# Attention in an encoder layer: the mask in the bias table, values on two column halves, the copy ahead of the exponentials, the sink as a column of scores

## The reference

```python
m = jnp.maximum(jnp.max(s, axis=-1, keepdims=True), sb)
p = jnp.exp(s - m)
denom = jnp.sum(p, axis=-1, keepdims=True) + jnp.exp(sb - m)
...
s = jnp.einsum('brjchd,bjkhd->bhjrck', qb, kb).astype(jnp.float32) * scale + bias[None]
s = jnp.where(valid[None, None], s, NEG_INF)
p = jax.nn.softmax(s, axis=-1).astype(v.dtype)
```

## Time and profile before

| | us |
|---|---|
| median of three runs | 2774.3 |
| the profiled execution, its own time | 2770.2 |
| its span (first to last instruction) | 2768.4 |
| TensorE matmuls busy in the span | 2559.1 |
| VectorE busy | 1794.7 |
| ScalarE busy | 1459.1 |
| GpSimd busy | 253.4 |

### The profile page before, as it was taken

How to read it: one execution, slowest core, us unless ns; L and a number is a source line. 1 busy time by engine, 2 the same in 40 slices (tenths; PEclk the granted TensorE clock), 3 DMA queues, 4 the chain that set the end, 5 groups by cost and what they waited for, 6 DMA issues and landing times. The chain is left out here.

```text
span 2768.4 us, 41766 instructions
## 1 busy us (share of the span) xinstructions
PE 2559.1 (92%) x15442; PEld 2295.4 (83%) x15442; DVE 1794.7 (65%) x2743; ACT 1459.1 (53%) x2028; POOL 253.4 (9%) x280
## 2 busy tenths in 40 slices
PE   7999978888797499999999999999999999999992
PEld 5888756666675499999999999999999999999991
DVE  6354277676556766676676666766767667667675
ACT  4332344444464356556565565565655655556553
POOL 0000033221000101001001010010110100101100
PEclk9999989999898699999999999999999999999996
DMA  4332212221542567677677676776776767767765
GB/s 151 124 122 92 102 44 72 71 76 50 212 144 95 203 229 250 222 255 247 225 254 245 234 245 223 255 245 225 254 240 241 242 227 252 247 226 251 243 239 210
DMA packets 97210, 538.73 MB, mean 195 GB/s; under 512 B 10800, under 2 KB 17200, under 8 KB 46576
## 3 DMA queue, kind: packets, MB, share of 16 engines
q1 hardware_dynamic: 89744, 511.82, 52.0%
q0 software_dynamic: 7392, 25.96, 4.2%
HBM read 499.99 MB, written 37.75 MB: 194 GB/s over the span
## 5 line engine op out<-in xcount | busy, mean ns | idle before, releaser
L1415 DVE TENSOR_TENSOR ex_w_lo<-ex_w,ex_w_hi 128x2048 fp32r<-128x2048 f32 x387 | 886.9, 2292 | 471.2 <-ACT ex_w_hi L1368 455.9
L1368 ACT ACTIVATE ex_w_hi<-ex_w 128x2048 fp32r<-128x2048 f32 x387 | 739.2, 1910 | 232.6 <-PE ex_down_ps L1519 114.1
L1501 PE MATMUL ex_gate_ps<-ex_xt,ex_w_hi 128*128 128x384 f32 x2048 | 594.3, 360 | 1.5 <-DVE ex_xt L1421 1.5
L1501 PE MATMUL ex_up_ps<-ex_xt,ex_w_hi 128*128 128x384 f32 x2048 | 592.1, 359 | 0.0
L1503 PE MATMUL ex_gate_ps<-ex_xt,ex_w_lo 128*128 128x192 f32 x2048 | 513.8, 251 | 0.0
L1503 PE MATMUL ex_up_ps<-ex_xt,ex_w_lo 128*128 128x192 f32 x2048 | 512.7, 250 | 0.0
L1503 PEld LDWEIGHTS ex_gate_ps<-ex_xt,ex_w_lo 128*128 128x128 f32 x2048 | 392.6, 192 | 0.6
L1503 PEld LDWEIGHTS ex_up_ps<-ex_xt,ex_w_lo 128*128 128x128 f32 x2048 | 391.2, 191 | 0.0
L1501 PEld LDWEIGHTS ex_gate_ps<-ex_xt,ex_w_hi 128*128 128x128 f32 x2048 | 385.8, 188 | 2.3 <-issue 1.7
L1501 PEld LDWEIGHTS ex_up_ps<-ex_xt,ex_w_hi 128*128 128x128 f32 x2048 | 384.3, 188 | 0.0
L630 ACT ACTIVATE at_probs<-at_probs,at_neg_top 128x384 f32<-128x384 f32 (+1 forms) x192 | 109.6, 572 | 178.7 <-DVE at_neg_top L684 109.7
(11 more groups left out here) (213 smaller groups left out, 4406.9 us busy)
## 6 DMA issues: line engine op xcount, KB each, us to landing
ex_w<-in_w_experts SPq DMA_DIRECT2D x387, 1024.0 KB, 4.8
pj_w<-in_w_in SPq DMA_DIRECT2D x54, 512.0 KB, 3.5
at_bias<-in_near_bias SPq DMA_DIRECT2D x8, 1536.0 KB, 7.3
pj_x<-in_x SPq DMA_DIRECT2D x12, 512.0 KB, 4.5
o_scratch<-at_o SPq DMA_DIRECT2D x24, 256.0 KB
mx_o<-o_scratch SPq DMA_DIRECT2D x12, 512.0 KB, 3.8
mx_x<-in_x SPq DMA_DIRECT2D x12, 512.0 KB, 4.5
acc_scratch<-mx_x SPq DMA_DIRECT2D x12, 512.0 KB, 5.4
```

The source lines that it names most:

```text
L1368: act.activation(w_hi[:, c % SLOTS, :], w[:, c % SLOTS, :], ACT.Copy).then_inc(hi_w, 1)
L1415: dve.tensor_tensor(w_lo[:, c % SLOTS, :], w[:, c % SLOTS, :], w_hi[:, c % SLOTS, :].bitcast(F32), ALU.subtract).then_inc(lo_w, 1)
L1501: nc.tensor.matmul(out[:, b, 0:2 * CAP], w_hi[:, slot, f], xt[:, k, :, :].rearrange("p h c -> p (h c)"), start=k == 0, stop=False)
```

## The change

- The table of biases that is put together on the host now holds -1e30 wherever a key is not seen. The mask tensor, its loads and GpSimd's additions are gone; VectorE waits for the load of the bias.
- The additions write to a new tile `raw`, eight rows of 385 elements, whose last column holds the head's sink. The exponential reads from `raw` and writes to `probs`; for a window unit it takes one column more, so its sum contains the sink. The separate subtraction, exponential and addition for the sink are gone. `probs` has four slots in place of six.
- The scores go around three PSUM banks in place of one for each head.
- Weighing is turned round: the 64 columns of a head's values are the stationary operand and the turned probabilities the moving one. The two heads write to PSUM partitions 0 to 63 and 64 to 127 of one bank, that is, each uses one half of the array's columns (`tile_position`), and their matmuls alternate.
- The result lies as features by queries, so ScalarE copies it to SBUF (`o_turn`), TensorE transposes it into another bank, and VectorE scales from there, one turn of the loop later (u-3).
- ScalarE's order is now: copy of the output of u-3, copy of the turned probabilities of u-1, exponentials of u.
- The turned values have one PSUM bank in place of two.

```diff
@@ -501,11 +501,10 @@
         N = len(units)
-        window_units = [sum(x[0].window for x in units[:u]) for u in range(N)]
...
-        PROBS, STATS, FLIPS, OUTS, BIASES, V_SLOTS = 6, 4, 6, 2, 3, 2 * len(V_TILES)
+        PROBS, STATS, FLIPS, BIASES, V_SLOTS, SCORES = 4, 4, 6, 3, 2 * len(V_TILES), 3
...
@@ -515,34 +514,31 @@
-        mask = sb("at_mask", [P, BIASES, NEAR_KEYS])
...
-        probs = sb("at_probs", [P, PROBS, NEAR_KEYS])
+        raw = sb("at_raw", [P, 2 * PAIRS, NEAR_KEYS + 1])
+        probs = sb("at_probs", [P, PROBS, NEAR_KEYS + 1])
         flipped = sb("at_flipped", [P, FLIPS, NEAR_KEYS])
...
-        score = [ps(f"at_score{h}", [P, 512]) for h in range(2)]
+        o_turn = sb("at_o_turn", [P, 2, P])
...
+        score = [ps(f"at_score{i}", [P, 512]) for i in range(SCORES)]
...
-        out_ps = [ps(f"at_out{i}", [P, 512]) for i in range(OUTS)]
-        v_ps = [ps(f"at_v{i}", [P, 512]) for i in range(2)]
+        mixed_ps = ps("at_mixed", [P, 512])
+        out_ps = ps("at_out", [P, 512])
+        v_ps = ps("at_v", [P, 512])
...
@@ -561,8 +559,6 @@
                              d["near_bias"][b.kind, strip][:, :, 0:b.keys]).then_inc(bias_in[slot], 16)
-                sp.dma_start(mask[:, slot, 0:b.keys],
-                             d["near_mask"][b.kind, b.strip][:, 0:b.keys]).then_inc(bias_in[slot], 16)
...
@@ -585,13 +581,6 @@
         def _(pool):
-            def mask_bias(n):
-                slot, keys = n % BIASES, blocks[near_start[n] // PAIRS].keys
-                pool.wait_ge(bias_in[slot], 32 * (n // BIASES + 1))
-                pool.tensor_tensor(bias[:, slot, :, 0:keys], bias[:, slot, :, 0:keys],
-                                   mask[:, slot, 0:keys].unsqueeze(1).broadcast_to([P, 2 * PAIRS, keys]),
-                                   ALU.add).then_inc(masked, 1)
...
             def stage_v(n):
...
@@ -609,9 +598,6 @@
                         stage_v(n)
-                for n in near_start:
-                    if u == (near_start[n - BIASES] + PAIRS + 2 if n >= BIASES else len(V_TILES)):
-                        mask_bias(n)
...
@@ -621,19 +607,14 @@
         def _(act):
-            for u in range(N + 1):
-                if u < N:
-                    b, r = units[u][0], u % STATS
-                    act.wait_ge(bounded, u + 1)
-                    for h in range(2):
-                        p = probs[:, (2 * u + h) % PROBS, 0:b.keys]
-                        act.activation(p, p, ACT.Exp, bias=neg_top[:, r, h:h + 1],
-                                       accum_out=sums[:, r, h:h + 1]).then_inc(exped, 1)
-                    if b.window:
-                        act.wait_ge(sink_at, window_units[u] + 1)
-                        act.activation(e_sink[:, r, :], at_sink[:, r, :], ACT.Exp).then_inc(sink_exped, 1)
-                if u >= 1:
...
+            for u in range(N + 3):
+                if u >= 3:
+                    v = u - 3
+                    act.wait_ge(weighed, v + 1)
+                    if v >= 2:
+                        act.wait_ge(o_turned, v - 1)
+                    act.activation(o_turn[:, v % 2, :], mixed_ps[:, 0:P], ACT.Copy).then_inc(o_copied, 1)
+                if 1 <= u < N + 1:
                     v = u - 1
...
@@ -641,34 +622,41 @@
                                    ACT.Copy).then_inc(copied[0], 1)
+                if u < N:
+                    b, r = units[u][0], u % STATS
+                    act.wait_ge(bounded, u + 1)
+                    pair, n = units[u][1], b.keys + b.window
+                    for h in range(2):
+                        act.activation(probs[:, (2 * u + h) % PROBS, 0:n],
+                                       raw[:, 2 * pair + h, NEAR_KEYS - b.keys:NEAR_KEYS - b.keys + n],
+                                       ACT.Exp, bias=neg_top[:, r, h:h + 1],
+                                       accum_out=sums[:, r, h:h + 1]).then_inc(exped, 1)
                 if u in v_step:
...
                     v_slots_free(act, n)
-                    act.activation(v_near[:, n % V_SLOTS, :], v_ps[n % 2][:], ACT.Copy).then_inc(v_copied, 1)
+                    act.activation(v_near[:, n % V_SLOTS, :], v_ps[:], ACT.Copy).then_inc(v_copied, 1)
...
             dve.tensor_scalar(neg_sink[:], sink[:], -1.0, None, ALU.mult).then_inc(negated, 1)
-            dve.wait_ge(negated, 1)
-            for u in range(N + 2):
+            dve.tensor_copy(raw[:, :, NEAR_KEYS:], sink[:].unsqueeze(2)).then_inc(negated, 1)
+            dve.wait_ge(negated, 2)
+            for u in range(N + 3):
                 if u < N:
...
                     if not b.window and pair == 0:
-                        dve.wait_ge(masked, b.number + 1)
+                        dve.wait_ge(bias_in[b.number % BIASES], 16 * (b.number // BIASES + 1))
                     for h in range(2):
                         dve.wait_ge(scored, 2 * u + h + 1)
-                        if 2 * u + h >= PROBS:
...
-                            dve.wait_ge(flipped_ps, 2 * (u - PROBS // 2 + 1))
                         if b.window:
...
                             add = bias[:, b.number % BIASES, 2 * pair + h, 0:b.keys]
-                        dve.tensor_tensor_reduce(out=probs[:, (2 * u + h) % PROBS, 0:b.keys],
-                                                 in0=score[h][:, 0:b.keys], in1=add, scale=1.0, scalar=-3.0e38,
+                        dve.tensor_tensor_reduce(out=raw[:, 2 * pair + h, NEAR_KEYS - b.keys:NEAR_KEYS],
+                                                 in0=score[(2 * u + h) % SCORES][:, 0:b.keys], in1=add, scale=1.0, scalar=-3.0e38,
                                                  op0=ALU.add, op1=ALU.max,
...
@@ -677,23 +665,13 @@
                                                  op0=ALU.mult, op1=ALU.min).then_inc(bounded, 1)
-                        dve.wait_ge(bounded, u + 1)
-                        dve.tensor_tensor(at_sink[:, r, :], neg_top[:, r, :], mine,
-                                          ALU.subtract).then_inc(sink_at, 1)
                     else:
...
                     dve.wait_ge(exped, 2 * v + 2)
-                    total = sums
-                    if units[v][0].window:
-                        dve.wait_ge(sink_exped, window_units[v] + 1)
-                        dve.tensor_tensor(den[:, r, :], sums[:, r, :], e_sink[:, r, :],
-                                          ALU.add).then_inc(summed, 1)
-                        dve.wait_ge(summed, window_units[v] + 1)
-                        total = den
-                    dve.reciprocal(rden[:, r, :], total[:, r, :]).then_inc(inverted, 1)
+                    dve.reciprocal(rden[:, r, :], sums[:, r, :]).then_inc(inverted, 1)
...
@@ -701,10 +679,10 @@
                                     flip_ps[1][:, 0:keys]).then_inc(copied[1], 1)
-                if u >= 2:
-                    v, r = u - 2, (u - 2) % STATS
+                if u >= 3:
+                    v, r = u - 3, (u - 3) % STATS
                     b, pair, bi = units[v]
-                    dve.wait_ge(weighed, v + 1)
+                    dve.wait_ge(o_turned, v + 1)
                     dve.wait_ge(inverted, v + 1)
...
@@ -714,7 +692,7 @@
-                    own = out_ps[v % OUTS][:, 0:2 * (P + HD)].rearrange("p (h x) -> p h x", h=2)[:, :, 0:HD]
+                    own = out_ps[:, 0:P].rearrange("p (h e) -> p h e", h=2)
                     dve.tensor_tensor(dst, own,
...
@@ -723,13 +701,12 @@
-            for u in range(N + 2):
+            for u in range(N + 3):
                 if u < N:
...
                     for h in range(2):
-                        if u >= 1:
...
-                            pe.wait_ge(added, 2 * (u - 1) + h + 1)
+                        if 2 * u + h >= SCORES:
+                            pe.wait_ge(added, 2 * u + h - SCORES + 1)
                         rows = slice(h * HD, (h + 1) * HD)
...
@@ -739,7 +716,7 @@
                             k = k_rows.rearrange("p (r c) -> p r c", c=GRID_W)[:, :, KEY_COL[b.strip]:KEY_COL[b.strip] + K_COLS]
-                        nc.tensor.matmul(score[h][:, 0:b.keys], q, k, start=True, stop=True).then_inc(scored, 1)
+                        nc.tensor.matmul(score[(2 * u + h) % SCORES][:, 0:b.keys], q, k, start=True, stop=True).then_inc(scored, 1)
                 if 1 <= u < N + 1:
...
@@ -1682,15 +1663,6 @@
     c["band"] = np.where(np.abs(j - P - i) <= P, 0.0, NEG).astype(np.float32)
-    masks = []
-    for kind in range(len(NEAR_ROWS)):
-        rows = GRID_H[kind]
-        for strip in range(STRIPS):
-            qr, qc, kr, kc = near_positions(kind, strip)
-            rs, cs = np.clip(qr - 4, 0, rows - KEY_ROWS), np.clip(qc - 8, 0, GRID_W - 16)
-            ok = (kr >= rs) & (kr < rs + KEY_ROWS) & (kc >= cs) & (kc < cs + 16)
-            masks.append(np.where(ok, 0.0, NEG).astype(np.float32))
-    c["near_mask"] = np.stack(masks).reshape(len(NEAR_ROWS), STRIPS, P, NEAR_KEYS)
     c["ident"] = np.eye(P, dtype=np.float32)
...
@@ -1704,13 +1676,16 @@
```

(18 more changed lines are left out.)

32 lines of the change are left out of this document (15 added, 17 removed).

## The result

Four runs of the changed kernel took 2662.1 to 2667.1 us, median 2663.0, against 2773.9 for the kernel before (four runs by then): a ratio of 0.9606, 95% interval 0.9592 to 0.962. The profiled execution took 2662.1 us (span 2660.3), 108.1 less than the profiled one of before. The forecast was 2685, range 2655 to 2732.

The account below looks back on a forecast made before the run. Bound: VectorE held during GpSimd's mask additions (68 us), then TensorE's work with waits. Stage 346.4 to 256.0 us (-90.4), +0.8 at the end: profiled 2770.2 to 2680.6, median 2685 us, range 2655 to 2732.

Parts of the forecast that it names:

- Mask in the table, -68: Attention stage: removing GpSimd's twelve mask additions and their loads saves 68 us, 57 of direct holding and 11 after it.
- the holds stay: Rival: VectorE's holds come from something other than the additions, such as GpSimd's remaining copies; 2753 us, chance 0.02.
- Sink as a column, 0: Window units: dropping the sink's exponential and two VectorE instructions gains 0, as VectorE has gaps in calm units.
- Three banks, 0: Scores on TensorE: a third PSUM bank lets scores start earlier, which TensorE's order already hides; 0.
- Halves: overlap with one record alone, 0.78, weighing 0.89: Weighing, 384 keys: two heads stream at once plus one record alone, 0.78 us instead of 1.33; whole weighing 0.89.
- the halves don't overlap: Rival, weighing: records on the column halves stream one after the other as before; 2728 us, chance 0.17.
- a change of half drains: Rival, weighing: each of 416 changes of half drains the array at 0.17 us, 71 us more; 2799 us, chance 0.03.
- One more form, 0.20: TensorE, each unit: one more switch of the array's form, taken as 0.20 us.
- the turn, 0.11: TensorE, each unit: one more turning, that of the output, 0.11 us; its wait for ScalarE's copy taken as covered.
- The wait kept of the calm gap, 0.15: Calm steps of 384 keys: 0.15 of the 0.21 us gap stays above TensorE's new floor, 2.76 to 2.91.
- At 256 keys, 2.25: Steps of 256 keys: floor 2.12 plus 0.13 kept, 2.25 us instead of 2.35; no reordering shortens the chain.
- One more step of pipeline, +0.8: End of the attention stage: one more step of pipeline costs 0.8 us once.

Follow-up runs that it names:

- experiments 1 to 3: Kernel before with only the mask put in the table: 2707.5 us; with additions cut by head: 2716.6; changed kernel plus GpSimd additions of zeros: 2734.0 us.
- experiment 6: Changed kernel with the weighing's loops exchanged, all key tiles of head 0 and then all of head 1: 2682.7 us.
- experiment 11: Changed kernel with the values' four turnings moved from behind the weighing to ahead of it: 2661.6 us.
- Experiment 4: Changed kernel with the weighing of before, no column halves, no turn and no copy of the output: 2691.8 us.
- experiment 7: Changed kernel with the exponentials of a unit back ahead of the copy of the unit before on ScalarE: 2689.9 us.

## Why the prediction was right, and where it was off

The forecast's case came about, column halves that overlap and holds that end. The time came 22 us under its number, 2 us outside that case's own range of 2665 to 2708 and inside the full one. The two halves of the forecast fared differently. The mask was forecast at -68 and measured at 63 to 71. All the rest was forecast at -22 (278.3 to 256.0 in the stage) and measured at -44 (2707.5 to 2663.0): right in kind, half in size. That the time still lies inside is owed to a lower end put 10 us below the case's own range, for which the prediction gives no term. By its steps:

- **Mask in the table, -68.** Measured 63 alone by the medians (65 by the stage), 71 as the cost of putting additions back. That the holds come with GpSimd's additions is shown by experiments 1 to 3, and that the holds stay is out.
- **Sink as a column, 0.** Measured 1.1 us, within what the runs tell apart.
- **Three banks, 0.** Right, with halves and without.
- **Halves: overlap with one record alone, 0.78, weighing 0.89.** The term was mis-sized: weighing to scores takes 0.80. The row of 12 records lasts 0.88 us; less one record's 0.28 that is 0.60 from the first start to the last, where eleven spacings of 0.111 would be 1.22: they go two by two with none left over, and weighing less the 0.11 above its records is 0.69, next to the 0.67 of full overlap. That the halves don't overlap, and that a change of half drains, are both out; alternation is what makes the overlap whole (experiment 6).
- **One more form, 0.20, and the turn, 0.11.** Together they measure 0.20 to 0.21 in place of 0.31, so a change of form to the halves costs about 0.1; experiment 11 gives 0.15 for one. The 0.20 was taken too high, between bounds of which the upper came from the filling of four score records.
The Trainium skill's rule that changing the tiling mode drains the engine while changing only the tile does not (TensorEngine Tiling, Key Properties) fits both experiment 11 (a change less, 0.15 us less in the step) and the free alternation of halves (12 records in 0.60 us from first to last start). The 2.38 for three column tiles from the Trainium skill (TensorE: Matmul & The Clock Gate, the measured speedups of its part on row and column tiling), which the prediction turned into an estimate of 0.84 us for the twelve records, would have been further off (0.69 measured) than the 0.78 from the row of the scores. In the sum it would have made 4 us more and not 5: 64 x 0.06, and nearly nothing at 256 keys.
- **The wait kept of the calm gap, 0.15.** Nearly right at 384 keys: what is left over 2.57 is 0.11, all of it values' turnings (two of 0.58 in ten steps). The reordering takes the waits away altogether.
- **At 256 keys, 2.25.** Too long, and wrong in its reason: it said that no reordering shortens the chain there. Experiment 4 has calm steps of 2.11 to 2.12 us at 256 keys, TensorE's floor of then, between these scalings; with halves they are 1.91.

```profile
...
487.69 0.29 DVE L686 TENSOR_TENSOR at_o<-at_out,at_rden 128x128 f32<-128x128 f32 x1
...
489.80 0.29 DVE L686 TENSOR_TENSOR at_o<-at_out,at_rden 128x128 f32<-128x128 f32 x1
...
491.92 0.29 DVE L686 TENSOR_TENSOR at_o<-at_out,at_rden 128x128 f32<-128x128 f32 x1
```

The average over all steps of 256 keys is 2.1 in the changed kernel.
- **One more step of pipeline, +0.8.** It shows at the other end: the first scaling begins 1.4 us later, and 0.2 us more follow the last one, 1.6 together.

The steps' terms: 64 x (2.91 - 2.68) = 15 and 31 x (2.25 - 2.10) = 5 make the 19 by which the stage was forecast too long (256.0 against 236.7). Most of the other 3 us is no step of the kernel: the forecast put the median 4.1 us above the profiled execution, as it lay before, and this time it lay 0.9 above (2663.0, 2662.1).

What the prediction did not see is that order and halves are worth more together. From 2706.4, the order alone takes 14.7 us and the halves alone (experiment 7) 16.5, together 43.4. The likely reason: TensorE's work (2.99 us a step, experiment 4) and the chain through ScalarE (2.87 a step with halves, experiment 7; without them its waits still add to TensorE's 2.99) are nearly as long as each other, so removing either lays the other bare.

Left open: whether a different hold would appear with other VectorE instructions than those of this stage; and what sets the 0.28 us after which the second half starts in experiment 6, since only the one order was tried.

## What to carry to other kernels

A small VectorE instruction that lasts microseconds (5.22 us here where 0.17 is usual) may be held: look for a GpSimd instruction that ends when it does, and if its work can be put into a table, or into shorter instructions, try that first. Where one side of two matmuls has only 64 columns, make it the stationary one and give each its half of the array's columns; alternate them, as issued one after the other they overlap only in part. When TensorE's work and a chain of waits are about as long, price the removal of both, not of each.

## What the runs showed that was not expected

- Cutting GpSimd's additions into eighths gave back 54 of the 63 us, though GpSimd's total work grew: 995 ns for an eighth against 6666 for the whole, 8.0 us in place of 6.7.
- Halving the moving columns from 128 to 64 left a record at 0.11 us; with 64 stationary and 128 moving columns, on two halves, two records go in that time.
- With the additions back, the stage's mean granted clock is 0.89, and 1.00 with them gone; but additions in eighths leave it at 1.00 from 355 to 385, where whole ones had 0.72.

```profile
...
346.00:652.00 306.00, 258.42 (x2054) 165.48 (x2052) 223.67 (x741) 182.84 (x579) 89.86 (x88) 0.89 0.20 63
```
